# Modulation rows in four column groups behind the mixer's input tiles, lag blocks on GpSimd, norm in steps

## The reference, cut to what matters

```python
silu_c, silu_cc = silu(c), silu(c_ctx)                    # two vectors of 1024
mod_x = silu_c  @ ada_w[i] + ada_b[i]                     # ada_w[i]: 1024 x 6144
mod_c = silu_cc @ ada_w[i] + ada_b[i]
sh1, sc1, g1, sh2, sc2, g2 = split(mod_x, 6)              # the same for the context
xn = rmsnorm(x, norm1_g[i]) * (1 + sc1) + sh1
# layer 0, chunk mixer
u, v = split(gelu(xn @ cm_w_in), 2)                       # 1024 x 2048
v = layernorm(v); v = einsum("hpq,bnqhd->bnphd", w_s, v) + b_s
y = (u * v) @ cm_w_out                                    # 1024 x 1024
x = x + g1 * y                                            # then the expert layer with sh2, sc2, g2
# layer 1, state-space mixer: matrices that depend on parameters alone
a = exp((lr + 1j * li) * step); bb = coef * b             # powers a^0..a^8, per group of 16 channels
# injection: a^m bb, readout: c a^m, lags: Re(c a^m bb) for 15 lags
```

## Time and profile before

| | |
|---|---|
| median of three runs | 4302.17 us (4298.98 to 4303.8) |
| the profiled execution: its time, its span | 4318.92 us, 4317.1 us |
| busy in the span: PE, DVE, ACT, POOL | 4140.5, 2899.5, 1557.4, 83.1 us |
| granted TensorE clock, mean | 0.971 |
| stage 1, from the end of the first block's last row sum to the first input tile | 768.95 to 903.26 us |
| stage 2, sixteen input tiles and what is beside them | 903.26 to 1082.50 us |
| stage 3, eight output tiles | 1082.50 to 1169.40 us |

### The profile page before, as it was taken

How to read it: one execution, slowest core, us unless ns; L and a number is a source line. 1 busy time by engine, 2 the same in 40 slices (tenths; PEclk the granted TensorE clock), 3 DMA queues, 4 the chain that set the end, 5 groups by cost and what they waited for, 6 DMA issues and landing times.

```text
span 4317.1 us, 62551 instructions
## 1 busy us (share of the span) xinstructions
PE 4140.5 (96%) x21410; PEld 3371.2 (78%) x21410; DVE 2899.5 (67%) x5248; ACT 1557.4 (36%) x2362; POOL 83.1 (2%) x92
## 2 busy tenths in 40 slices
PE   7899899999899999999999999999998899999998
PEld 7697789356585788888888888888747788888886
DVE  6342275867689777777689777777451698777776
ACT  5201051112106644444307444444322147444443
POOL 0000000000000000000000000000310000000000
PEclk9899999989899999999999999999989999999999
DMA  5213355643254566656552566656663433555654
GB/s 178 65 48 103 106 179 159 208 147 91 87 189 137 159 189 188 189 189 189 190 186 78 181 189 187 189 188 195 175 217 100 155 124 126 188 189 188 189 189 136
DMA packets 209752, 686.43 MB, mean 159 GB/s; under 512 B 36528, under 2 KB 46784, under 8 KB 208464
## 3 DMA queue, kind: packets, MB, share of 16 engines
q1 hardware_dynamic: 173584, 627.88, 45.9%
q0 software_dynamic: 11712, 47.29, 3.6%
q10 hardware_dynamic: 24320, 9.37, 0.8%
HBM read 659.36 MB, written 24.05 MB: 158 GB/s over the span
## 4 chain that ended last, share of the span: by engine, by line
PE 89%; DVE 7%; DMA 2%; ACT 2%; issue 1%; SPq 0%; DVEq 0%; ACTq 0%
PE psum L976 24%; PE psum L962 15%; PE psum L573 8%; PE psum L964 8%; PE psum L1042 7%; PE psum L619 4%; PE psum L1078 4%; PE psum L643 4%; PE psum L892 1%; DMA ring<-in_w 1%; PE psum L871 1%; PE psum L603 1%; PE psum L941 1%; PE psum L1194 1%; PE psum L1029 1%; PE psum L1254 1%
## 5 line engine op out<-in xcount | busy, mean ns | idle before, releaser
L976 PE MATMUL psum<-rows_split_odd,coef_split 128*128 128x512 f32 x2400 | 589.7, 395 | 2.1 <-DVE rows_split_odd L2110 1.1
L2115 DVE TENSOR_REDUCE work<-psum 128x256 f32<-128x512 f32 x356 | 246.3, 692 | 502.6 <-PE psum L964 502.6
L976 PE MATMUL psum<-rows_split,coef_split 128*128 128x512 f32 x2208 | 532.0, 390 | 0.3 <-issue 0.3
L976 PEld LDWEIGHTS psum<-rows_split_odd,coef_split 128*128 128x128 f32 x2400 | 436.8, 188 | 104.4 <-issue 4.9
L962 PE MATMUL psum<-input_split,rows_split 128*128 128x512 f32 x1424 | 508.2, 397 | 1.2 <-DVE rows_split L2110 1.2
L962 PE MATMUL psum<-input_split,rows_split_odd 128*128 128x512 f32 x1424 | 504.3, 393 | 0.0
L976 PEld LDWEIGHTS psum<-rows_split,coef_split 128*128 128x128 f32 x2208 | 402.1, 188 | 81.5 <-issue 0.9
L2110 DVE TENSOR_TENSOR rows_split_odd<-ring,rows_split_odd 128x1024 fp32r<-128x1024 f32 x378 | 460.0, 1217 | 6.5 <-ACT rows_split_odd L1276 6.5
L1460 ACT ACTIVATE work<-work 128x256 f32<-128x256 f32 x356 | 149.0, 419 | 858.6 <-DVE work L2115 858.6
L1276 ACT ACTIVATE rows_split_odd<-ring 128x1024 fp32r<-128x1024 f32 x378 | 398.6, 1055 | 164.2 <-PE psum L976 161.8
L2110 DVE TENSOR_TENSOR rows_split<-ring,rows_split 128x1024 fp32r<-128x1024 f32 x362 | 440.3, 1217 | 4.4 <-ACT rows_split L1276 4.4
(11 more groups left out here) (391 smaller groups left out, 5405.6 us busy)
## 6 DMA issues: line engine op xcount, KB each, us to landing
ring<-in_w SPq DMA_DIRECT2D x420, 512.0 KB, 3.6
ring<-in_u SPq DMA_DIRECT2D x384, 512.0 KB, 3.5
ring<-in_v SPq DMA_DIRECT2D x384, 512.0 KB, 3.5
scratch_cm<-work POOLq DMA_DIRECT2D x16, 512.0 KB, 3.4
scratch_inj<-stage ACTq DMA_DIRECT2D x16, 512.0 KB, 2.9
arena<-scratch_inj POOLq DMA_DIRECT2D x7, 1024.0 KB, 7.5
arena<-scratch_parked POOLq DMA_DIRECT2D x4, 1024.0 KB, 9.3
arena<-scratch_lags POOLq DMA_DIRECT2D x32, 128.0 KB, 6.0
```

The source lines that it names most:

```text
L976: last = mm(bank(2 + 2 * i + f), CFR[:, b, c, P * i:P * i + P], parts[:, v, 512 * f:512 * f + 512], start=(first and c == 0 and v == 0), s ...
L2115: dve.tensor_reduce(AC[:, b, :], bank(b).rearrange("p (x t) -> p t x", x=2), AX, ALU.add)\
```

## The change

- The stationary operand `CSP` is `CS` padded with zeros to 32 columns. `row_part` puts the four products (two slots, two halves of 512 columns) into four 32-partition groups of one PSUM bank, so even and odd slots give two partial sums. `turn_row` turns a row with four matmuls of four columns, adding the two partial sums by the matrix `PART`; ACT copies a row out as 128 x 512.
- Only rows 0 and 1 (shift and scale of the mixer's input) are made in stage 1. Rows 2 to 5 come in stage 2: the weight stream brings one mixer slot and two modulation slots in turn, and `last_rows(t)` follows each input tile.
- `prepare` runs once in stage 1 and after each of the input tiles 0 to 14; none is left in stage 3.
- POOL makes the lag blocks (`lag_part`, six instructions of 960 elements a block) and, between its real and imaginary part, issues the store of the readout block before (`store_readout(b - 1)`, which waits for `cm_ready` b); `WCM` has two buffers. DVE keeps injection and readout.
- `parameters` runs to its end inside the first block's down projection; 96 copies of 64 elements are 12 of 512.
- The mixer's input is normed in eight instructions of 512, and ACT applies shift and scale in sixteen of 256.

```diff
@@ gpsimd
+            def lag_part(b, out, first, second, op):
+                ptt(out, power(first[0]), mat(first[1]), ALU.mult)
+                PL.do(ptt(WTL, power(second[0]), mat(second[1]), ALU.mult))
+                return ptt(out, out, WTL, op)
+            pool.wait_ge(sem("parameters_ready"), 1)
+            for b in range(NPREP):
+                if b >= 2:
+                    pool.wait_ge(sem("lags_turned"), b - 1)
+                PL.do(lag_part(b, WW[b % 2][:, :, 0, :], (0, 0), (1, 1), ALU.subtract))
+                if b:
+                    store_readout(b - 1)
+                last = lag_part(b, WW[b % 2][:, :, 1, :], (0, 1), (1, 0), ALU.add)
+                last.then_inc(sem("lags_ready"), 1)
...
@@ tensor
+            def row_part(b, w, k, f):
+                q = 2 * (k % 2) + f
+                return mm(bank(b)[32 * q:32 * q + 32, :], CSP[:, k, :],
+                          ring[:, w % RING, 512 * f:512 * f + 512],
+                          start=(k < 2), stop=(k >= 6))
...
-            for q in range(6):
-                ada(q)
-                if q == 0:
-                    rowsum(SQA, 8, 512)
-                if q >= 6 - IN_ADA:
-                    prepare(q - (6 - IN_ADA))
+            ada(0)
+            rowsum(SQA, 8, 512)
+            prepare(0)
+            ada(1)
+            L.slots += 16
+            pe.wait_ge(sem("modulation_operands"), 3)
+            pe.wait_ge(sem("lags_evacuated"), 1)
+            for q in range(2):
+                L.take("row_copied")
+                L.mark(turn_row(row_at(q), MR[:, q, :]), "row_turned")
...
-                if t in IN_TILES:
-                    prepare(IN_ADA + IN_TILES.index(t))
+                if t < NPREP - 1:
+                    prepare(t + 1)
...
@@ tensor, last_rows(t), called after beside(t)
+                for i in range(2):
+                    w, k = w0 + 3 * t + 1 + i, (2 * t + i) % 8
+                    arrived(w)
+                    for f in range(2):
+                        last = row_part(7, w, k, f)
...
@@ vector
+            prepare_injection(0)
             L.do(norm(X[:, :, 0:S], col("norm_final", 0, 8), X[:, :, 0:S], 8, 1.0 / D))
...
-            L.do(tt(H, X, over(R2, 8, 1), ALU.mult))
+            for k in range(KD_):
+                L.mark(tt(H[:, k, :], X[:, k, :], R2, ALU.mult), "inputs_scaled")
...
             gain(4)
             gain(5)
-            prepare_lags(first + 7)
+            prepare_injection(14)
             for h in range(4):
                 gate(h)
             gain(6)
             gain(7)
+            prepare_injection(15)
+            prepare_readout(14)
```

More of the change, by code:

```diff
@@ L858, in _, with turn_row @@
             rowsum(SQF, 8, S)
-            L.take("cond_silu")
+            pe.wait_ge(sem("modulation_operands"), 2)
             w0 = L.slots
+            def row_part(b, w, k, f):
[3 more added lines that the diff above has]
+                          start=(k < 2), stop=(k >= 6))
+            def turn_row(off, row):
+                to = PS(off, 2, 4, 2).rearrange("p f u c -> p u f c")
+                for u in range(4):
+                    last = mm(to[:, u], row[:, P * u:P * u + P], PART, start=True, stop=True, skip_group_check=True)
+                return last
             def ada(q):
-                if q >= 2:
-                    pe.wait_ge(sem("ada_evacuated"), q - 1)
                 for k in range(8):
@@ L915, in modulation @@
                         for f in range(2):
-                            last = mm(bank(4 + f)[0:2, :], CS[:, k, :],
-                                      ring[:, L.slots % RING, 512 * f:512 * f + 512], start=(k == 0), stop=(k == 7))
+                            last = row_part(4, L.slots, k, f)
                             if f == 0:
@@ L1614, in _ @@
             L.lin += 16
-            for b in range(OUT_FIRST, NPREP):
-                prepare(b)
             others(8)
@@ L2005, in parameters @@
                 ts(A2C[:, 0, :], PW[:, 8, 1, :], -1.0, None, ALU.mult)
[L2006 to L2021 removed]
+                L.give(cp(A2C[:, 1, :], PW[:, 8, 1, :]), "parameters_ready")
             RE, IM = ((0, 0), (1, 1), ALU.subtract), ((0, 1), (1, 0), ALU.add)
@@ L2241, in peer @@
                 L.give(ins, "acc_evacuated")
-            first = IN_ADA
             def gain(h):
@@ L2256, in gate @@
                 L.mark(tt(Z[:, h, :], Z[:, h, :], MIXED[:, h, :], ALU.mult), "gated")
-            for b in range(first, first + 5):
+            prepare_readout(1)
+            for b in range(2, 10):
                 prepare(b)
+                if b == 6:
+                    row_sum(2)
             dve.wait_ge(sem("v_turned_evacuated"), 8)
@@ L2266, in _ @@
             L.mark(dve.reciprocal(VAR, VAR), "var")
-            prepare_readout(first + 5)
+            row_sum(3)
+            prepare_readout(10)
             L.take("rstd")
@@ L2273, in _ @@
             ins.then_inc(sem("v_normed"), 1)
-            prepare_lags(first + 5)
+            prepare(11)
             L.take("mixed")
@@ L2292, in _ @@
             gain(7)
-            for h in range(4, 7):
+            prepare_injection(15)
+            prepare_readout(14)
+            for h in range(4, 8):
                 gate(h)
-            prepare_injection(OUT_FIRST)
-            gate(7)
+            prepare_readout(15)
+            dve.wait_ge(sem("rows_added"), 3)
+            L.do(scaled(0, 1))
             L.lin += 16
```

248 lines of the change are left out of this document (144 added, 104 removed).

## The result

The changed kernel takes 4333.7 us (median of five runs, 4328.5 to 4335.6), the kernel before 4303.8 beside it (five runs, 4299.0 to 4315.1): a ratio of 1.0065, 95% interval 1.0049 to 1.0082. It is slower by 30 us where I had forecast 24 faster. That is the side of rival 1, and 7 us short of its 4341.

The account below looks back on a forecast made before the run. PE was taken as the bound, busy 96% of the span and 89% of the chain. Stage 1 -94, stage 2 +101 and stage 3 -31 gave -24 us, so 4302.2 became 4278; own range 4264 to 4293, 8 in 10 4258 to 4341.

Parts of the forecast that it names:

- rival 1: DVE and GpSimd take turns at SBUF: +39 us in total, 4341; chance 0.24 in full, 0.09 by half.
- Stage 1: Modulation rows and prepares before the first input tile: 134.3 us before, 40.5 after, a gain of 94.
- The parameters' tail: Parameter copies inside the down projection: bounds 4 and 8 us, last `add_x` up to 2.4 late; taken as nothing.
- Stage 2 without the turns: Input tiles, prepares and rows, DVE and GpSimd not blocking each other: 179.2 us before, 280 after, a cost of 101.
- the half: Stage 2's row slots at 0.89 us, half of 1.77, between no overlap and all four groups at once; 28 us.
- rival 2: All four column groups run at once: 14 us less in stage 2, -39 in total, 4263; chance 0.13.
- Rival 3: Column groups do not overlap: 28 us more in stage 2, 4 in stage 1; +8 in total, 4310; chance 0.12.
- The tail: End of stage 2, PE waiting on DVE's list after tiles 13 and 14: 5.3 and 16.3 us, sum 21.6.
- Stage 3: Last input tiles, now without prepares: 86.9 us before, 56 after, a gain of 31.
- The gate builds: Expert layer's first pass, where a row product stands between builds: bounds 0 to 7 us of gain, taken as 0.
- The late rows: The three rows of the scan, which lie behind DVE's scan: taken as 0.
- The base: Start of the sum: -24 us taken off the median 4302.2; the profiled execution, 4318.9, lay 16.7 above it.

Follow-up runs that it names:

- lags on DVE: Changed kernel with the lag blocks made on DVE again and POOL only issuing stores: 4303.4 us, ratio 1.0013 to the kernel before.
- reordered with GpSimd: Changed kernel with DVE's list in the order PE waits, lags on GpSimd: 4309.3 us, 1.0013; the same with lags on DVE: 4270.7 us, 0.9923.
- the memsets: Changed kernel with GpSimd's six arithmetic instructions a block replaced by memsets of 1920 elements, lag values left out: 4284.9 us, ratio 0.9974 to the kernel before.
- the late start: Changed kernel with GpSimd's first lag block waiting until the mixer's input is normed: 4330.8 us, ratio 1.0069 to the kernel before.

## Why the prediction was wrong

- **The step that failed** is "DVE's share falls to twelve instructions of 0.69 a block, 8.3 us, hidden in 16", with GpSimd's six taken as hidden beside them. They are not beside them but in turn: DVE's products of a block take 16.9 us (269.7 / 16 from the groups) in place of 8.3, and the tiles of the steady part are 19.5 us apart in place of 16. GpSimd's duration was nearly right, 2.17 us on average for 2.2, but a part of the 2.17 is its own waiting; alone it is 1.96. I had written the rule down as rival 1 and given it a third of the chance because no row showed it; two prices from rows (6 x 2.2 added, 6 x 1.156 saved) already said that, if the rule holds, the port carries 6.3 us more a block after the move than before it. Shown by three pairs: GpSimd reading against writing (48 us in the sum of the table, 49 in the medians, with GpSimd's six instructions a block the only difference), changed against lags on DVE (43 to 45 in the table), and reordered with GpSimd against without (40.9 in the table, 39 in the medians).
- **Rival 1's price** was too high. Forecast 11 at the start and 52 behind, 63 in all; against the memsets it is 6.7 to the first tile (54.3 and 47.6; the late start alone gives back 3.3) and 40 in stage 2 (312.8 and 272.9), 48 in all. From the sixth to the thirteenth tile the changed kernel needs (1037.58 - 900.91)/7 = 19.5 us a tile, not 21.5. GpSimd's own duration explains most of it: 8.3 + 11.7 = 20.0 us a block by an estimate from its rows where DVE is idle, where I had taken 8.3 + 13.2. That the total came within 7 us of 4341 is partly luck: the price was 15 too high, and the other errors below went the other way.
- **Stage 1**: first tile at 822.8, 13.4 late. By PE's timeline: 6.1 before the row sum (788.87 for 782.75; with GpSimd's late start it begins at 784.13, so 4.7 of it is the norm beside GpSimd), 1.3 in the row sum, 1.2 back in the prepare, 4.8 for the second row's slots (15.8 from 801.71; they came more slowly than one in 1.9 us), 2.5 in the hand-over.
- **The parameters' tail** was a term that I put at nothing. From the down projection's first matmul to the first row product of stage 1 PE needs 84.2 us in both traces of before and 87.5 in the changed kernel (87.5 to 89.1 in all its variants): 3.4 us that lie ahead of the stages and of the table. Most of it is the wait before the last row sum, 4.76 where it was 2.59.
- **Stage 2 without the turns**: 280 forecast. The version with the forecast's DVE list, the memsets, took 272.9; that the lags on DVE gave 279.5 and 276.1 is a coincidence in size, for DVE does more there. Its tiles were 16.0 forecast and (1008.57 - 818.83)/12 = 15.8 measured. The 32 slots of rows: 28 us forecast, 25.1 measured. But my reason for the half was wrong: all four groups do run at once, as rival 2 had it (0.50 a slot at the upper clock, 0.44 forecast there), and it is the lower clock, in eleven of sixteen places, that brings the mean to 0.78. Rival 3 is out. The Trainium skill has 2.38 times the rate for three such tiles (TensorE: Matmul & The Clock Gate, "Packing small matmuls — row/col tiling"); the 3.5 times for four groups here (1.77 against 0.50) agrees with it in kind.
- **The tail** was seen but not weighed as an edit. Forecast waits 5.3 and 16.3; in the changed kernel 4.83 and 4.83 + 9.72. With the memsets the same waits stand at 9.7 and 8.7, so they are the order's and not the turns'. Reordering took 23 to 26 us out, and with the lags on DVE, where more of the list was moved, about 33 (396.8 to 363.0 is 33.8, by the medians 33).
- **Stage 3**: 56 forecast, 56.09. **The gate builds**: taken at 0; from the expert layer's first matmul of 256 columns on weights to its next part 249.7 against 249.4. **The late rows** beside the scan: 0 taken, 63.6 against 61.0; over all changed versions it is 61 to 64.
- **The base** was a second, independent error. I worked out -24 from windows of one execution and took it off the median of others. That execution was slow by 16.3 in just these stages against the second (415.1 and 398.8); the two other traces in the old order lie between, at 412.6 and 410.7. Against the first trace the memsets gain 23.8 in them, which is the forecast's 24; against the second 7.5, and by the medians 12. So even with the port left alone the forecast of 4278 would have been missed: 4284.9 with the memsets, and 4303.4 with the lags on DVE.

What stays open: the medians put the lags-on-DVE version 6 us above the kernel before, its two traces put it 2 to 4 ahead of the faster trace of before in these stages. The 3.4 us ahead of the stages and up to 3 in the late rows take that back; what is left is within the spread of single traces, whose stages vary by up to 16 us. Open too is what makes the granted clock differ between two executions of one kernel. Not tried was GpSimd's arithmetic at a time when DVE has nothing to multiply, as in stage 3.

## What to carry to other kernels

Work moved from DVE to GpSimd is little relief while DVE multiplies two SBUF operands: the two add up, and here GpSimd's 2.0 us (alone) replaced DVE's 1.16 for the same 960 elements. Give GpSimd work that only writes, or, as far as two pairs of instructions in one trace show it, work beside DVE's PSUM reads. Before moving work off a busy engine, order its list by what the bound engine waits for next: here this was worth 33 us, and the move cost 39. And before taking a difference from windows of one trace, look at the granted clock of these very windows in a second one.

## What the runs showed of the hardware

- GpSimd's one-input copies (1.06 to 1.23 us) slow DVE's two-input products from 0.69 to 0.92 to 1.05; its memsets of 1.7 us don't. DVE products that read PSUM kept their time where they lay beside GpSimd's products (two of 512 elements in 1.41 us, twice, in the kernel before with GpSimd's lag blocks). Two DVE tensor-scalars of 1024 elements with a single tensor input took 2698 ns on average for 810 before, and ended behind two of GpSimd's products (5.32 us from 995.62).
- The delay is not bounded by one GpSimd instruction. Twelve DVE products of the changed kernel took 3.4 to 4.8 us: each ended behind the two of GpSimd's that follow the issue of a store and have no semaphore between them. Before the store the same two lines held DVE for one instruction at a time, and no product took over 2.7. What makes the difference is not shown.
- GpSimd waits as well. Its first two instructions take 1.82 and 1.83 us where DVE is idle, and up to 2.17 and 2.28 where a DVE product is under way.
- Products in four 32-column groups cost 0.50 us a slot (0.93 at the lower clock) where the same products one behind the other cost 1.77: a factor of 3.5.
- The 64-column matmuls of the second layer run at either clock from one execution to the next, 7.36 or 13.91 us for 64 of them; of the fourteen traces eight showed the faster form and six the slower. In the two traces of the kernel before this makes 12 us.
